# Hybrid attention and mixture-of-experts step: adaLN modulation with the condition vectors as the stationary operand

## The reference

```
m  = silu(cvec) @ w_ada + b_ada           # cvec is c_ctx or c; m is cut into six vectors of 1024
sh1, sc1, g1, sh2, sc2, g2 = split(m, 6)
h  = x * (1 + sc1) + sh1                  # shift 0 and scale 1, per column of D
qkv = h @ w_in                            # then attention, w_out, LayerNorm, mixture of 16 experts
```

## Time and profile before

| | |
|---|---|
| runs | 1994.87, 1997.33, 1999.80 us; median 1997.33 us |
| profiled execution | span 1995.6 us; no other time is given for it |
| busy share of the span | PE 97%, PEld 67%, DVE 83%, ACT 69%, POOL 9% |
| mean granted TensorE clock | 0.980 |
| bytes moved | 636.33 MB, mean 319 GB/s |

### The profile page before, as it was taken

How to read it: one execution, slowest core, us unless ns; L and a number is a source line. 1 busy time by engine, 2 the same in 40 slices (tenths; PEclk the granted TensorE clock), 3 DMA queues, 4 the chain that set the end, 5 groups by cost and what they waited for, 6 DMA issues and landing times.

```text
span 1995.6 us, 25171 instructions
## 1 busy us (share of the span) xinstructions
PE 1931.0 (97%) x9620; PEld 1334.2 (67%) x9620; DVE 1660.0 (83%) x1636; ACT 1384.3 (69%) x1625; POOL 188.3 (9%) x99
## 2 busy tenths in 40 slices
PE   9999899975999999999999999999999999999998
PEld 8999667653666666666666666666666666666665
DVE  3777566677988989898989898988989898989897
ACT  3222456635787787878787878787787878787876
POOL 0000212122010101010110101010101010110100
PEclk9999799986999999999999999999999999999999
DMA  9543501155999999999999999999999999999994
GB/s 384 199 174 154 183 27 57 50 179 197 392 358 392 378 393 375 373 389 363 398 362 394 347 406 352 402 353 392 375 381 379 367 388 365 398 361 395 351 395 174
DMA packets 102934, 636.33 MB, mean 319 GB/s; under 512 B 11584, under 2 KB 21824, under 8 KB 30112
## 3 DMA queue, kind: packets, MB, share of 16 engines
q1 hardware_dynamic: 97696, 618.19, 79.2%
q0 software_dynamic: 4832, 16.50, 3.0%
q10 hardware_dynamic: 288, 0.03, 0.0%
HBM read 620.02 MB, written 13.88 MB: 318 GB/s over the span
## 4 chain that ended last, share of the span: by engine, by line
PE 75%; ACT 1%; DVE 0%; issue 0%; DVEq 0%
PE ps L1558 16%; PE ps L1557 16%; PE ps L1562 16%; PE ps L1574 8%; PE ps L1575 8%; PE ps L1579 8%; PE ps L1537 1%; PE ps L1528 0%; ACT place L1667 0%; ACT place L1663 0%; ACT place L1670 0%; DVE place L1722 0%; ACT place L1615 0%; ACT place L1665 0%; DVE place L1738 0%
## 5 line engine op out<-in xcount | busy, mean ns | idle before, releaser
L721 DVE TENSOR_TENSOR place<-ring,place 128x2048 fp32r<-128x2048 f32 x527 | 1224.3, 2335 | 144.3 <-ACT place L717 141.2
L717 ACT ACTIVATE place<-ring 128x2048 fp32r<-128x2048 f32 x528 | 1009.6, 1916 | 310.5 <-PE ps L1562 234.0
L1557 PE MATMUL ps<-place 128*80 128x512 f32 x1408 | 560.9, 398 | 1.8 <-DVE place L1678 1.8
L1558 PE MATMUL ps<-place 128*80 128x512 f32 x1408 | 555.5, 395 | 0.0
L1562 PE MATMUL ps<-place 128*80 128x512 f32 x1408 | 381.3, 392 | 0.0
L1562 PEld LDWEIGHTS ps<-place 128*80 128x80 f32 x1408 | 208.2, 148 | 115.8 <-issue 0.7
L1558 PEld LDWEIGHTS ps<-place 128*80 128x80 f32 x1408 | 209.1, 149 | 107.0 <-issue 0.5
L1574 PE MATMUL ps<-place 128*80 128x512 f32 x704 | 280.5, 398 | 0.0
L1557 PEld LDWEIGHTS ps<-place 128*80 128x80 f32 x1408 | 208.5, 148 | 107.4 <-DVE place L1678 2.0
L1575 PE MATMUL ps<-place 128*80 128x512 f32 x704 | 277.1, 394 | 0.0
L1579 PE MATMUL ps<-place 128*80 128x512 f32 x704 | 190.4, 392 | 0.0
(11 more groups left out here) (209 smaller groups left out, 1774.4 us busy)
## 6 DMA issues: line engine op xcount, KB each, us to landing
ring<-in_w_exp SPq DMA_DIRECT2D x528, 1024.0 KB, 6.9
ring<-in_w_late SPq DMA_DIRECT2D x16, 1024.0 KB, 11.1
ring<-in_w_in SPq DMA_DIRECT2D x12, 1024.0 KB, 6.3
ring<-in_w_ada SPq DMA_DIRECT2D x7, 1024.0 KB, 10.2
ring<-in_w_out SPq DMA_DIRECT2D x4, 1024.0 KB, 5.9
place<-in_near_bias SPq DMA_DIRECT2D x16, 256.0 KB, 3.2
ring<-in_xT SPq DMA_DIRECT2D x4, 640.0 KB, 8.9
place<-in_x SPq DMA_DIRECT2D x5, 512.0 KB, 6.1
```

Of the source, the lines that this page charges most:

```text
L717: eng.activation(wH[:, n % SPLITS, :], ring[:, slot("exp", n), :], ACT.Copy).then_inc(wh_done, 1)
L721: eng.tensor_tensor(wL[:, n % SPLITS, :], ring[:, slot("exp", n), :], wH[:, n % SPLITS, :].bitcast(F32), ALU.subtract).then_inc(chunk_used, 1)
L1557: eng.matmul(out, xH[:, e % 2, kk, :], w, start=(kk == 0), stop=False)
L1558: eng.matmul(out, xL[:, e % 2, kk, :], w, start=False, stop=False)
```

## The change

The operands of the early modulation change places. The two condition vectors (32 columns with zeros, `silu_w`) are the stationary operand and the weights stream, 256 columns at a time. The eight k-tiles go to four groups of 32 columns of the array in turn (`q = QUAD * (k % QUADS)`), so that the PSUM bank holds four partial sums, in rows on partitions 0, 32, 64 and 96. DVE copies the bank to SBUF (`copy_row`), and PE multiplies the copy, as stationary operand, by `gather`, a 128 x 2 matrix with ones where the partition modulo 32 is 0 or 1 (`ada_turn`); this adds up the four groups and brings the columns onto the partitions. `early` adds the bias as before. PE takes row n+1 before it turns row n. The low half of `w_in` chunk 0 now stands between the copy and the addition of chunk 6 on DVE.

`w_in` chunk 0 is asked for ahead of modulation chunks 6 and 7 and the last token chunk. `project_first` takes the first two column tiles together: for each token tile, as it comes, the products of both.

```diff
-STREAM = 96
+QUAD = 32
+QUADS = 4
+ROW_COLS = 256
...
         for j in range(KT // 2):
+            if j == KT // 2 - 1:
+                stream += [("in", 0)]
             stream += [("ada", 2 * j), ("ada", 2 * j + 1), ("x", j)]
         for i in range(GROUPS):
-            stream += [("in", 3 * i + s) for s in range(3)] + [("late", LATE_PER * i + j) for j in range(LATE_PER)]
+            stream += [("in", 3 * i + s) for s in range(i == 0, 3)] + [("late", LATE_PER * i + j) for j in range(LATE_PER)]
...
-                for n in range(EARLY):
+                def ada_row(n):
                     if n:
                         arrived(eng, "ada", n)
                     else:
                         eng.wait_ge(half_landed, 16)
+                        arrived(eng, "ada", 0)
                     if n >= 4:
                         eng.wait_ge(ada_added, n - 3)
                     w = weights(slot("ada", n))
+                    for k in range(KT):
+                        q = QUAD * (k % QUADS)
+                        mm = eng.matmul(ps[q:q + QUAD, 4 + n % 4, 0:ROW_COLS], silu_w[:, k, :], w[:, k, :],
+                                        start=(k < QUADS), stop=(k >= KT - QUADS))
+                    mm.then_inc(ada_used, 1)
+
+                def ada_turn(n):
+                    if n == 0:
+                        eng.wait_ge(gather_landed, 16)
+                    eng.wait_ge(ada_copied, n + 1)
                     for j in range(2):
-                        if n == 0 and j == 1:
-                            arrived(eng, "ada", 0)
-                        for k in range(KT):
-                            mm = eng.matmul(ps[:, 4 + n % 4, j * STREAM:(j + 1) * STREAM], w[:, k, j * P:(j + 1) * P],
-                                            silu_w[:, k, :], start=(k == 0), stop=(k == KT - 1))
-                    mm.then_inc(ada_used, 1)
+                        mm = eng.matmul(ps[:, 4 + n % 4, ROW_COLS + 2 * j:ROW_COLS + 2 * j + 2],
+                                        ada_rows[:, n % 2, j * P:(j + 1) * P], gather, start=True, stop=True)
+                    mm.then_inc(ada_turned, 1)
+
+                for n in range(EARLY):
+                    ada_row(n)
+                    if n:
+                        ada_turn(n - 1)
+                ada_turn(EARLY - 1)
...
+                def project_first():
+
+                    wh, wl = halves(0)
+                    cols = [slice(g * P, (g + 1) * P) for g in range(2)]
+                    eng.wait_ge(whi_done, 1)
+                    for k in range(KT):
+                        eng.wait_ge(x_split, k + 1)
+                        for g in range(2):
+                            for b, (t0, t1) in enumerate(HALVES):
+                                out = ps[:, 2 * g + b, 0:TOK // 2]
+                                eng.matmul(out, wh[:, k, cols[g]], xH[:, k, t0:t1], start=(k == 0), stop=False)
+                                eng.matmul(out, wh[:, k, cols[g]], xL[:, k, t0:t1], start=False, stop=False)
+                    eng.wait_ge(wlo_done, 1)
+                    for g in range(2):
+                        for k in range(KT):
...
+                        mm.then_inc(qk_ready, 1)
...
+                def copy_row(n):
+                    eng.wait_ge(ada_used, n + 1)
+                    if n >= 2:
+                        eng.wait_ge(ada_turned, n - 1)
+                    eng.tensor_copy(ada_rows[:, n % 2, :], ps[:, 4 + n % 4, 0:ROW_COLS]).then_inc(ada_copied, 1)
+
                 def early(n):
                     m, pair = n % 2, n // 2
-                    eng.wait_ge(ada_used, n + 1)
-                    src = ps[:, 4 + n % 4, 0:2 * STREAM].rearrange("p (j c) -> p j c", j=2)[:, :, 0:2]
+                    eng.wait_ge(ada_turned, n + 1)
+                    src = ps[:, 4 + n % 4, ROW_COLS:ROW_COLS + 4].rearrange("p (j c) -> p j c", j=2)
...
                 for k in range(0, KT, 2):
-                    early(k)
+                    copy_row(k)
                     if k == KT - 2:
                         low(0)
+                    early(k)
+                    copy_row(k + 1)
                     early(k + 1)
```

More of the change, by code:

```diff
@@ L114, in build @@
         lam_s = take(8)
+        gather = take(2)
         silu_c = take(2 * KT).rearrange("p (k v) -> p k v", k=KT)
@@ L199, in chain @@
             nc.vector.wait_ge(dve_own.sem, dve_own.k)
-        silu_w = rtmp.rearrange("p b n -> p (b n)")[:, 0:KT * STREAM].rearrange("p (k v) -> p k v", k=KT)
         junk = rtmp.rearrange("p b n -> p (b n)")
+        silu_w = junk[:, 0:KT * QUAD].rearrange("p (k v) -> p k v", k=KT)
+        ada_rows = junk[:, KT * QUAD:KT * QUAD + 2 * ROW_COLS].rearrange("p (b n) -> p b n", b=2)
         lam_in = kout[:, 0, :].rearrange("p (m d) -> p m d", m=4)
@@ L214, in build @@
         silu_spread = sem("silu_spread")
+        gather_landed = sem("gather_landed")
+        ada_copied = sem("ada_copied")
+        ada_turned = sem("ada_turned")
         ada_added = sem("ada_added")
@@ L306, in project @@
                     for k in range(KT):
-                        if n == 0:
-                            eng.wait_ge(x_split, k + 1)
                         for out, (t0, t1) in zip(outs, HALVES):
@@ L316, in project @@
                     mm.then_inc(qk_ready, 1)
+                def project_first():
[12 more added lines that the diff above has]
+                        for k in range(KT):
+                            for b, (t0, t1) in enumerate(HALVES):
+                                mm = eng.matmul(ps[:, 2 * g + b, 0:TOK // 2], wl[:, k, cols[g]], xH[:, k, t0:t1], start=False,
+                                                stop=(k == KT - 1))
+                        mm.then_inc(qk_ready, 1)
                 def values(i, t, high=True, low=True):
@@ L337, in _ @@
                 for i in range(GROUPS):
-                    for g in range(4):
+                    if i == 0:
+                        project_first()
+                    for g in range(2 * (i == 0), 4):
                         project(i, g)
@@ L363, in _ @@
                 eng.dma_start(badaT, a["b_ada"]).then_inc(c_landed, 16)
+                eng.dma_start(gather, a["gather"]).then_inc(gather_landed, 16)
                 eng.wait_ge(c_landed, 32)
@@ L1786, in constants @@
         "iota": np.arange(TOK, dtype=np.float32),
+        "gather": (np.arange(P)[:, None] % QUAD == np.arange(2)[None, :]).astype(np.float32),
         "ident": np.eye(P, dtype=np.float32),
```

## The result

The changed kernel takes **2002.12 us** (median of 10 runs, 1998.64 to 2003.51), the one before, on the same chip and between the same runs, 1996.96 (10 runs). The ratio is **1.0024**, with a 95% interval of 1.0016 to 1.0032. The forecast was 2002.0: no change that a measurement of this kernel can tell, on the slow side. The runs did tell it in the end, +0.24%.

The account below looks back on a forecast made before the run. PE and the transfers were taken to run level up to about 40 us, then PE alone to bound; +3.9 (later projection) - 2.3 (waits) + 2.2 and + 0.9 (low clock) = +4.7 us on 1997.33, so 2002.0, range 1995.5 to 2008.0.

Parts of the forecast that it names:

- What bounds: Head: PE and transfers neck and neck to about 40 us, then PE alone; only its start without pause can shift.
- The first projection, +3.9 at full clock and +0.9 for a low one: Head: first projection starts at 40.5 instead of 36.57, 3.9 us later; low clock on row 6, turns 5 and 7 adds 0.9.
- the links behind row 6: Head: copy 6 ends 36.45, ACT's w_in rounding 37.1, low half 0 39.3, turn 7 40.5, then the first projection.
- everything end on chunk 7: Head's transfers: ada 7, on which everything ends, lands at 33.0, 2.5 us later, because w_in moved forward.
- my 1.0 and 0.6: Modulation on PE: a row's 16 instructions take 1.0 us, a turn 0.6 us.
- The waits for x, -2.3: First projection: PE's 2.3 us of waits, mainly for the last two x tiles, are gone.
- The clock at the projection, +2.2: First projection: clock low when it begins, costing 2.0 to 2.5 us, taken as +2.2.
- The late chunk at 47.3: Behind the early chunks: first late chunk still reaches DVE at 47.3, with the same bytes ahead as before.
- That the groups don't run side by side: Rival, modulation rows: a chunk costs PE 4.04 us; +7.1, with low clock +9.3, 2004.4 to 2006.6; chance 0.20.
- The clock low through the whole head: Rival, head: rows of 2.0 and turns of 1.2 us; +6.0, 2003.3; chance 0.14, half of it beyond 6 us.
- The transfers as the only bound: Rival, head: DVE and ACT keep up, projection starts 1.5 earlier without waits; -3.8, 1993.5; chance 0.06.
- What would show it: Head signs: rows about 1 us, copy 7 near 39.4, first projection 40 to 42.5 without tile waits, PEclk 0.50 there.

Follow-up runs that it names:

- a: Changed kernel with w_in chunk 0 asked for in its old place, behind all modulation chunks; 2001.43 us, ratio 1.0022 to the kernel before.
- c: Changed kernel with idle matmuls into an unused bank between rows and turns on PE; 1998.86 us, ratio 1.0012 to the kernel before.
- e: Changed kernel with all eight k-tiles of a row in one column group, so nothing runs side by side; 2008.12 us, ratio 1.0051.
- d: Kernel before with project_first alone, the first two column tiles taken together; 1994.97 us, ratio 0.9988.
- i: Changed kernel with w_in 0 behind modulation chunk 7, rows and copies in pairs, low half 0 last, no idle matmuls; 1995.04 us, ratio 0.9988.
- j: Same changes as i, plus idle matmuls between rows and turns and 14 more before the first projection; 1993.24 us, ratio 0.9979.
- b: Changed kernel with DVE's low half 0 of w_in moved behind the last two x tiles; 1999.42 us, ratio 1.0015.
- k: Kernel before with project_first, and w_in chunk 0 asked for ahead of the last x chunk; 1994.35 us, ratio 0.9988.
- g: Same as h, with idle matmuls between rows and turns; 1998.82 us, ratio 1.0005.
- h: Same as i, but with low halves 1 and 2 one place further ahead of the late chunks; 1997.34 us, ratio 1.0004.

## Why the prediction was right, and where its terms were off

The forecast was +4.7 us; the medians gave +5.2, the trace +5.5. The chain was as forecast; part of the fit was luck, as points 2 and 6 say.

1. *What bounds.* Right. The change moved one moment, the start from which PE works without a pause, and everything behind moved with it by the same 5.5.
2. *The first projection, +3.9 at full clock and +0.9 for a low one.* +5.46 in all, and the links behind row 6 are right: copy 6 ended at 37.8 (36.45), ScalarE's rounding at 38.4 (37.1), low half 0 at 40.7 (39.3), turn 7 at 42.0 (40.5). That row 6 began at 30.46 (30.5) is luck. I had it wait for its transfer; it stood right behind turn 4, whose copy had waited behind VectorE's tiles, and a, where its chunk is asked for a megabyte earlier, starts it no sooner. In the forecast I had followed that chain for the last pair only. The transfer was not far behind: in c, with shorter rows, row 6 waited for it until 31.00. Nor did everything end on chunk 7, as I had said: row 7 was done at 35.3 and PE then stood still for 2.48 us. The term that was mis-sized is the low clock: I had put under half of its price, 0.9 of 2.2, on row 6 and turns 5 and 7. The clock was low on all of them, and it cost about 1.6 (5.46 - 3.9). A row took 1.93 and a turn 1.01; c shows what a row takes at full clock, 1.07, and e has turns of 0.60, so my 1.0 and 0.6 were right for that clock.
3. *The waits for x, -2.3.* Right: no wait between the tiles of the projection, and d shows the part alone, 1.8 plus the 0.41 by which its projection started later.
4. *The clock at the projection, +2.2.* Right in size (2.2 in the changed kernel; 2.7 in i against j), and shown by taking it away: j's projection, with no pause over 0.54 in the 10 us ahead of it, runs at full pace from its first matmul, c's too. But I had counted on a low clock only from the projection on, and halfway on the links ahead of it; it was low from the first row. The Trainium skill, TensorE: Matmul & The Clock Gate, section HAM oscillation, names this pattern: bursts of matmuls shorter than the waits behind them drop the clock. The changed kernel agrees with it (turn 6 is 1.01 us of work between pauses of 2.48 and 2.32). i does not: its pieces of work lasted 1.93 us or more, no pause in the 10 us ahead of the projection was over 0.69, and the pace stayed low. There the measurement decides.
5. *The late chunk at 47.3.* Wrong: it came at 49.59. SyncE could not ask for the late chunks before 40.72, since the first of them takes the slot that low half 0 releases, and the queue ran dry (share 0.90 between 30 and 40). I had followed the queue's bytes and not this release. It cost nothing, because VectorE waits for PE behind it anyway: low half 1 at 58.73 waited for PE. In b it was later still and cost nothing either.
6. *Rivals.* That the groups don't run side by side falls by e against c, 3.64 and 1.07. Had it been so, e shows what it would have cost: +12.8 by the third tile, more than the 9.3 that I gave it, since I left out the low clock of the first two rows (9.98 us for both) and took 3.44 for a row of 3.64. The clock low through the whole head is what came true; I had it at a chance of 0.14 and at 2003.3, 1.2 above the median. So the time was that of the forecast and the state of the clock that of this rival. The measured shift lies between the two (+4.7 and +6.0), since the low rows and turns on the chain cost 1.6, neither 0.9 nor 2.2. The transfers as the only bound fall by the pauses of 2.3 to 2.6 us that ended with copies.
7. *What would show it.* I had named PEclk at 0.50 ahead of the projection. It stayed at 1.00; the intervals of 0.267 us are what showed the low clock. I had also said that a measurement tells about 0.3% from no change; ten runs of each kernel told 0.24%. Two small slips, neither of which moves the forecast: half of the 0.14 of that rival is 0.07, where I added 0.08; and x 2 was asked for 3.1 us later than before (19.21 and 16.08), not 2.

Asked for early, `w_in` chunk 0 was not used early (a), as the prediction had it. So the change is one good part, the projection tile by tile, worth about 2.2 (d), and one that frees PE at the price of two more links per chunk through VectorE, which PE then waits for: 7.7 with its low clock (5.5 + 2.2). j shows that these links and this clock can be taken out again. What is then left against the kernel before, 0.21%, is no more than k has with the old modulation, as far as the runs can tell (1993.24 and 1994.35 by the medians, 215.43 and 214.95 by the scores): a gain of the new modulation itself is not shown.

## What to carry to other kernels

Where an engine that you relieve stands level with the transfers, its freed time is idle time: count what new hand-overs the saving brings, and where the last one stands in the other engine's queue. A pause of PE ahead of a dense stretch can cost more than its length, for the stretch may then start at half pace (g: a pause of 1.92 us, and 2.8 us more for the 64 matmuls than in j): fill it, or shift work so that there is none. And when an order is mended, keep the work that waits for the late engine behind the work that doesn't (h against i: 3.1 us).

## What the runs showed of the hardware

- Four column groups of plain fp32 matmuls run side by side almost fully: 16 instructions of 256 columns in 1.07 us, 3.64 in one group (c, e), 3.4 times. The Trainium skill, TensorE: Matmul & The Clock Gate, section Measured speedup vs the span model, has 2.38 for three column tiles and no entry for four. The estimate of 1.4 us for a row that I made from it was 0.3 too long for the 1.07 measured at full clock, and the measurement decides.
- In these traces the record of the granted clock does not show a low level that holds from the start. In the changed kernel the projection's first matmuls start 0.267 us apart while the record says 1.00, as in i above; in e and g, where the clock had first been high, the same interval comes with 0.50. e, then the changed kernel, in 2 us:
```profile
48.00:50.00 2.00, 1.80 (x7) 1.78 (x8) 0.31 (x2) 0.56 (x2) 0.00 (x0) 0.50 0.99 418
50.00:52.00 2.00, 2.00 (x10) 2.00 (x9) 1.13 (x3) 1.67 (x3) 0.00 (x0) 0.50 1.04 438
```
```profile
44.00:46.00 2.00, 2.00 (x9) 2.00 (x9) 1.93 (x4) 1.70 (x3) 0.00 (x0) 1.00 1.01 426
```
  The same 9 or 10 matmuls in 2 us at 0.50 and at 1.00. e alone shows it too: its rows go from 6 instructions in 2 us to 11 under an unchanged record.
```profile
10.00:12.00 2.00, 2.00 (x6) 0.89 (x5) 0.00 (x0) 0.00 (x0) 0.00 (x0) 1.00 1.07 449
...
14.00:16.00 2.00, 2.00 (x11) 1.03 (x10) 0.41 (x1) 0.00 (x0) 0.00 (x0) 1.00 1.00 417
```
  In a head, read the clock from the distance of equal matmuls.
- Pauses of 1.58, 1.92 and 2.73 us (c, g, e) were followed by a fall of the clock to 0.50, those of 0.54 and 1.22 in j were not. But the kernel before had one of 1.63 without a fall, and g and h both had one of 2.88, with a fall in g alone. So the length of the last pause alone does not decide; what else does stays open here.
- Whether a head ran its first row at half pace went with the pause ahead of that row: 2.59 to 3.21 us in the changed kernel, a, b, e, h and i, all at half pace; 0.82, 0.20 and 0.23 in c, g and j, all at full pace. The idle matmuls of c, g and j also filled later pauses, so how much of the rest of the head hangs on this first one was not separated.
